# Twelve tiles of projection A per modulation block; the gate's modulation in the recurrence's weight stream

## The reference

```python
c_act = jax.nn.silu(c)                        # (1, 2048)
mod   = c_act @ ada_w[l] + ada_b[l]           # (1, 3*2048): shift | scale | gate
h     = rms_norm(x, pre_gain[l]) * (1.0 + scale) + shift
proj  = h @ w_in[l]                           # r,k,v | lora | z_a | conv, z_b | g_a, g_b
y_a   = (rwkv7_mix(pa, ...) * silu(z_a)) @ p_a[l]
y_b   = (short_conv_mix(pb, conv_w[l]) * silu(z_b)) @ p_b[l]
m     = sigmoid(g_a) * y_a + sigmoid(g_b) * y_b
x     = x + gate * rms_norm(m @ w_out[l], post_gain[l])
```

## Time and profile before

| | us |
|---|---|
| median of 3 runs (2261.99 to 2267.79) | 2263.99 |
| the profiled execution | 2260.67 |
| its span (first to last instruction) | 2259.1 |
| PE busy in it | 2211.5 |
| DVE busy | 1538.2 |
| ACT busy | 1106.0 |

### The profile page before, as it was taken

The page is one execution under the profiler, slowest core; times in us unless marked ns, Lnnn a source line. Parts: engine busy times, 40 slices in busy tenths (PEclk is TensorE's granted clock), DMA queues, the critical chain, the costliest instruction groups (busy, mean ns, idle before and its releaser), DMA issues.

```text
span 2259.1 us, 40660 instructions
## 1 busy us (share of the span) xinstructions
PE 2211.5 (98%) x15228; PEld 1869.7 (83%) x15228; DVE 1538.2 (68%) x2326; ACT 1106.0 (49%) x1741; POOL 123.3 (5%) x128
## 2 busy tenths in 40 slices
PE   6999999999999999999999999999999999999998
PEld 3688888888888888888888887888888888888887
DVE  5868776767776567678666666665566566566767
ACT  2344454555544456465455555544444454445454
POOL 0011000000000010120000002000000000000202
PEclk9999999999999999999999999999999999999999
DMA  9989744334334466665634435555555555555552
GB/s 377 390 314 352 248 138 136 124 132 132 122 122 134 151 228 219 219 205 177 205 131 131 141 126 191 184 178 194 178 194 183 190 177 195 182 189 183 182 184 84
DMA packets 116079, 424.86 MB, mean 188 GB/s; under 512 B 13200, under 2 KB 13456, under 8 KB 115696
## 3 DMA queue, kind: packets, MB, share of 16 engines
q1 hardware_dynamic: 107136, 390.68, 51.0%
q0 software_dynamic: 8816, 32.38, 4.1%
HBM read 414.62 MB, written 8.39 MB: 187 GB/s over the span
## 4 chain that ended last, share of the span: by engine, by line
PE 89%; DVE 5%; ACT 2%; DMA 2%; issue 1%; SPq 0%; DVEq 0%; ACTq 0%
PE ps L2102 48%; PE ps L2103 23%; PE ps L2220 5%; PE ps L2481 3%; PE ps L2482 1%; DMA raw<-in_stream 1%; DVE acc L1301 1%; DVE wlo L1270 1%; PE ps L2634 1%; ACT whi L700 1%; PE ps L2155 0%; DMA xt<-in_x 0%; PE ps L2156 0%; PE ps L2157 0%; DVE ysq L1536 0%
## 5 line engine op out<-in xcount | busy, mean ns | idle before, releaser
L2102 PE MATMUL ps<-acts,whi 128*128 128x512 f32 x3456 | 1254.4, 405 | 3.1 <-DVE stage L1276 1.6
L1270 DVE TENSOR_TENSOR wlo<-raw,whi 128x1024 fp32r<-128x1024 f32 x647 | 809.0, 1260 | 597.0 <-ACT whi L700 594.9
L700 ACT ACTIVATE whi<-raw 128x1024 fp32r<-128x1024 f32 x671 | 703.8, 1057 | 707.1 <-PE ps L2103 629.7
L2103 PE MATMUL ps<-acts,wlo 128*128 128x256 f32 x3456 | 967.5, 280 | 0.0
L2102 PEld LDWEIGHTS ps<-acts,whi 128*128 128x128 f32 x3456 | 649.3, 188 | 171.5 <-issue 9.1
L2103 PEld LDWEIGHTS ps<-acts,wlo 128*128 128x128 f32 x3456 | 652.9, 189 | 4.5 <-issue 3.3
L2102 PE MATMUL ps<-hidn,whi 128*128 128x512 f32 x1280 | 451.5, 397 | 2.3 <-DVE s L1276 1.8
L2103 PE MATMUL ps<-hidn,wlo 128*128 128x256 f32 x1280 | 357.2, 279 | 0.0
L2102 PEld LDWEIGHTS ps<-hidn,whi 128*128 128x128 f32 x1280 | 239.9, 187 | 63.9 <-DVE s L1276 4.2
L2103 PEld LDWEIGHTS ps<-hidn,wlo 128*128 128x128 f32 x1280 | 241.3, 188 | 0.5 <-issue 0.5
L700 ACT ACTIVATE half<-ps 128x256 f32<-128x256 f32 (+1 forms) x341 | 129.6, 386 | 77.7 <-PE ps L2103 50.7
(11 more groups left out here) (340 smaller groups left out, 2024.2 us busy)
## 6 DMA issues: line engine op xcount, KB each, us to landing
raw<-in_stream SPq DMA_DIRECT2D x735, 512.0 KB, 3.8
graw<-in_ada_gate POOLq DMA_DIRECT2D x32, 512.0 KB, 5.5
gate_dram<-stage POOLq DMA_DIRECT2D x32, 128.0 KB, 2.5
gab<-gate_dram POOLq DMA_DIRECT2D x8, 512.0 KB, 5.5
xt<-in_x SPq DMA_DIRECT2D x1, 2048.0 KB, 10.2
xt<-in_x POOLq DMA_DIRECT2D x1, 2048.0 KB, 9.4
ple_dram<-pr__111 POOLq DMA_DIRECT2D x4, 512.0 KB, 3.8
pj<-ple_dram POOLq DMA_DIRECT2D x1, 2048.0 KB, 12.4
```

Of the source, the lines that this page charges most:

```text
L700: return nc.scalar.activation(dst, src, ACT.Copy)
L1270: tt(wlo[:, n % SPLIT, :], raw[:, g % RAW, :], whi[:, n % SPLIT, :].bitcast(F32), ALU.subtract).then_inc(raw_used, 1)
L2102: mm(ps[bank + n][:, :], whi[:, n0 % SPLIT, c:c + P], act[:, off + kt + k, :], start=kt + k == 0, stop=False)
L2103: ins = mm(ps[bank + n][:, 0:T], wlo[:, n0 % SPLIT, c:c + P], act[:, off + kt + k, 0:T], start=False, stop=kt + k == last)
```

## The change

**Opening.** A block of the stream has 28 tiles instead of 22: 15 A (12 before), one P (four before) and 12 W (six before). With the six after the last block that makes 42 W tiles. They are 21 units of two tiles (`UNITS`: column block, quarter of the channels, pair of banks), and a pair of banks passes from one column block to the next: after the last unit of a partial sum ACT copies it to `rkvz` (`part_out`, 2 x 512 columns), and PE's next unit in these banks waits for that. The rest of projection A is 22 tiles in five pieces (`REST`: 6, 6, 4, 4 and 2 tiles); DVE puts each piece into `wt` and adds it to the part in `rkvz`, four small instructions more per piece. Neither the zeroing matmuls nor the copy of a row and its transposition are left: a P tile is now eight matmuls of a 128 x 128 piece of the tile with one column of `cact`, and the sum over `acc` eight of the same kind, straight into columns of bank 6. `modulation` stands one A tile earlier on DVE, `rows_lo` is in two halves, and ACT's `h` and `acts` go in two pairs.

**Gate.** The 32 tiles are part of the main stream, each just ahead of the weight tile that DVE splits at one of 32 chosen slots of the recurrence (`GATED`: three or four per stage, one in the last). `gate_sums` adds one with two DVE instructions of 512 columns just before that split, and `gate_columns` sums `gacc` on PE (4 matmuls) at slot 9 of stages 1, 3, 5 and 7. POOL loads none of them any more.

```diff
-WITH_ADA = "AAAAPAWPAWAPWAPWAAWAAW"
+WITH_ADA = "AAAA" + 6 * "AW" + "PAW" + 2 * "AAW" + "WWW"
 TAIL = 3
-OPEN = FIRST + 3 * WITH_ADA + "W" * 2 * EARLY
+UNITS = ((0, 0, 0), (1, 0, 1), (2, 0, 2), (3, 0, 0), (4, 0, 1), (5, 0, 2),
...
+REST = ((1, 2), (2, 2), (3, 4), (4, 4), (5, 6))
...
+GATED = {-1: (10, 20, 26), **{i: (5, 15, 21, 25) for i in (0, 2, 4, 6)}, **{i: (4, 10, 22, 26) for i in (1, 3, 5)}, 7: (4,)}
+GATES = sorted(LEAD + STAGE * (i + 1) + k for i, at in GATED.items() for k in at)
+GATE_AFTER = [WB0 + h // 2 - 1 + AHEAD for h in GATES]
...
-            with gp.Fori(0, 8) as i:
-                for m in range(4):
-                    gp.wait_ge(s.gate_used, i * 4 + (m + 1))
-                    gp.dma_start(graw[:, m, :], ada_gate[bass.ds(i * 4 + m, 1), :, :].rearrange("a p n -> (a p) n")
-                                 ).then_inc(gate_in[m], 16)
...
+            def part_out(w):
+
+                u = (w - SPLIT) // 2
+                if w % 2 == 0 or u not in ENDS[:-1]:
+                    return
+                blk_, _, at = UNITS[u]
+                act.wait_ge(quarters, used(WA0 + 2 * u + 1))
+                for n in range(2):
+                    p = blk_ % 2 * 4 + 2 * n
+                    copy(rkvz[:, p:p + 2, wa_at[blk_]:wa_at[blk_] + T], ps[2 * at + n][:, :].rearrange("p (a t) -> p a t", a=2)
+                         ).then_inc(s.part_out, 1)
...
-                for j in range(8):
-                    split(WA0 + 8 * b + j + AHEAD)
-                    if j < 7 and m < 2 * KT:
-                        dst = gacc[:, m // KT * CW:m // KT * CW + CW]
-                        dve.wait_ge(gate_in[m % 4], 16 * (m // 4 + 1))
-                        dve.wait_ge(s.gate_used, m + 4)
-                        stt(dst, graw[:, m % 4, :], cact[:, m % KT:m % KT + 1], dst, ALU.mult, ALU.add).then_inc(s.gate_used, 1)
...
+                for n in range(4):
+                    first_half(wt[:, n, :], n, 4 * EARLY + 4 * r + n)
+                for n in range(4):
+                    dve.wait_ge(evac_done, 4 * EARLY + 4 * r + n + 1)
+                    dst = rkvz[:, blk_ % 2 * 4 + n, wa_at[blk_]:wa_at[blk_] + T]
+                    V.do(tt(dst, dst, wt[:, n, :], ALU.add))
+                V.wait()
...
+            def gate_sums(m):
+                g, row = gate_place(m), m % 8 * 2
+                v = raw[:, g % RAW, :]
+                dve.wait_ge(raw_ready[g % RAW], 16 * (g // RAW + 1))
...
+                    stt(gacc[:, :], v[:, 0:512], cact[:, row:row + 1], gacc[:, :], ALU.mult, ALU.add).then_inc(s.gate_used, 1)
+                dve.wait_ge(s.gate_used, m + 1)
+                stt(gacc[:, :], v[:, 512:CW], cact[:, row + 1:row + 2], gacc[:, :], ALU.mult, ALU.add).then_inc(raw_used, 1)
...
                 def at(k):
-                    slot(LEAD + STAGE * (i + 1) + k)
+                    h = LEAD + STAGE * (i + 1) + k
+                    if h in GATES:
+                        gate_sums(GATES.index(h))
+                    slot(h)
...
-                for n in range(2):
-                    ins = mm(ps[6 + n][0:1, :], cact[:, j:j + 1], raw[:, g % RAW, n * 512:(n + 1) * 512], start=first, stop=False)
+                for n in range(8):
+                    ins = mm(ps[6][:, n:n + 1], raw[:, g % RAW, n * P:(n + 1) * P], cact[:, j:j + 1], start=first and n == 0, stop=False)
                 ins.then_inc(s.ada_used, 1)
...
-            for n in range(2 * EARLY):
-                mm(ps[n][:, :], ident, half[:, 0:2, :].rearrange("p a t -> p (a t)"), start=True, stop=False)
             sum_squares(0, scr0)
...
-            pe.wait_ge(s.gate_used, 36)
-            for n in range(KT):
-                ins = mm(ps[5][:, n:n + 1], gacc[:, n * P:(n + 1) * P], ones[:, 0:1], start=True, stop=True)
-            ins.then_inc(s.gate_ps, 1)
...
+            def gate_columns(p):
+                pe.wait_ge(raw_used, RAW + gate_place(8 * p + 7) + 1)
+                for n in range(4):
+                    ins = mm(ps[6][:, 448 + 4 * p + n:449 + 4 * p + n], gacc[:, n * P:(n + 1) * P], ones[:, 0:1], start=True, stop=True)
+                ins.then_inc(s.gate_ps, 1)
```

More of the change, by code:

```diff
@@ L173, in lay_out @@
         for kind, _, n in opening(b):
-            opened.append((w_a[n % (2 * EARLY) // 2, 2 * b + n % 2] if kind == "W" else shift_scale[b + 1][n])[None])
+            opened.append((w_a[UNITS[n // 2][0], 2 * UNITS[n // 2][1] + n % 2] if kind == "W" else shift_scale[b + 1][n])[None])
+    starts = [0] + [g + 1 - WB0 for g in GATE_AFTER]
     stream = [
         *opened,
-        w_a[EARLY:].reshape(-1, P, CW),
+        *[w_a[blk, j:] for blk, j in REST],
         w_in[:, 3 * DA:za].reshape(2, 8, P, P).transpose(0, 2, 1, 3).reshape(2, P, CW),
-        blocks(np.concatenate(conv_and_gates, 1)),
+        *[part for m in range(len(GATES)) for part in (w_b[starts[m]:starts[m + 1]], ada_gate[m:m + 1])],
+        w_b[starts[-1]:],
         *[blocks(p) for p in p_ab],
@@ L225, in opening, with in_stream, gate_place @@
     for n, kind in enumerate(kinds):
-        yield kind, at + n, 2 * EARLY * b + tile if kind == "W" else ada
+        yield kind, at + n, WITH_ADA.count("W") * b + tile if kind == "W" else ada
         ada, tile = ada + (kind != "W"), tile + (kind == "W")
+def in_stream(g):
+    return g + sum(after < g for after in GATE_AFTER)
+def gate_place(m):
+    return GATE_AFTER[m] + 1 + m
 def taken(g):
@@ L539, in block_of_two_layers @@
         eye = con[:, C_EYE:C_EYE + CH]
+        wa_at = [(OR, OK, OV, OZ)[blk_ // 2] for blk_ in range(8)]
         def per_chunk(c):
@@ L1340, in _ @@
                            ).then_inc(raw_used, 1)
-                    if n == 3 and b < 3:
+                    if n == 2 and b < 3:
                         modulation(b)
-                    if n == 8 and b < 3:
-                        rows_lo(b)
+                    if n in (3, 4) and b < 3:
+                        rows_lo(b, n - 3)
                     if n == 13 and b < 3:
                         rows_scaled(b + 1)
-            for w in range(8 * EARLY, 8 * EARLY + AHEAD):
+            for w in range(OPENED, OPENED + AHEAD):
@@ new lines, in _ @@
+            for r, (blk_, first) in enumerate(REST):
+                for j in range(first, 8):
+                    split(WA0 + w + AHEAD)
+                    w += 1
+                if r == 0:
+                    last, _, at = UNITS[-1]
+                    dve.wait_ge(quarters, 4 * (SPLIT + OPENED))
+                    dve.wait_ge(s.part_out, 2 * len(ENDS) - 2)
+                    for n in range(2):
+                        dst = rkvz[:, last % 2 * 4 + 2 * n:last % 2 * 4 + 2 * n + 2, wa_at[last]:wa_at[last] + T]
+                        tt(dst, ps[2 * at + n][:, :].rearrange("p (a t) -> p a t", a=2), dst, ALU.add).then_inc(evac_done, 2 * EARLY)
+                for n in range(4):
+                    first_half(wt[:, n, :], n, 4 * EARLY + 4 * r + n)
[4 more added lines that the diff above has]
+                V.wait()
@@ L1661, in _ @@
             centred(HT - 1)
+            gate_post()
             split(PAB0 + AHEAD)
```

179 lines of the change are left out of this document (90 added, 89 removed), and 3 rows, old and new, of the table UNITS.

## The result

| | before | changed |
|---|---|---|
| median of four runs each, us | 2262.99 (2259.95 to 2267.79) | 2239.19 (2238.54 to 2243.14) |
| the profiled execution, us | 2260.67 | 2238.54 |
| its span, us | 2259.1 | 2236.9 |

The ratio is 0.990, 95% interval 0.989 to 0.992: the kernel is faster by about 24 us in the medians and by 22.1 us in the profiled executions. Predicted were 2245 and a range of 2234 to 2256.

The account below looks back on a forecast made before the run. PE, busy for 2211.5 of 2259.1 us, was taken as the bound. Terms -20.5 - 3.0 + 3.6 + 2.0 + 0.4 = -17.5 on 2260.7 gave 2243.2, raised to 2245 for the runs' median; range 2234 to 2256.

Parts of the forecast that it names:

- rival 1: As forecast: PE the longest of three in the opening, 2245 us, own range 2238 to 2251; chance 0.62.
- the term -20.5: Change in when PE finishes projection A's 64 tiles, from 267.35 to 246.9 us; bounds -29 and -10.
- Start of the first W tile: In the opening: the first W tile starts at 49.5 us (48.58 before), bounds 45.5 and 52.
- The 42 W tiles and six short groups: Opening: 42 W tiles at 2.88 us, 121.0, plus three P tiles and three sums over `acc` at 2.0 each, 12.0.
- Waits and clock, 3 us: PE's waits and low clock in the opening's blocks: 3 us together, bounds 0 and 11; opened tiles done at 185.5.
- The other 22 tiles: Rest of projection A: 22 tiles at 2.79 us, 61.4 in all, ending at 246.9 us.
- Between projection A and the recurrence: Column sums and low clock go, 5.1 us; a wait for `xz` returns 2.1: -3.0, bounds -5.1 and 0.
- The recurrence: Column sums in four groups +3.6, gate sums' stalls +2 (bounds 0 and +12), `gate_post` behind the last stage +0.4 us.
- rivals, 2: No start penalty and no waits in the opening: 2231 to 2237 us; chance 0.13.
- Rival 3: DVE or the queues become the bound in the blocks, 41 us each instead of 38.6: 2252 to 2259; chance 0.13.
- Rival 4: The change does nothing: low clock after each of 11 one-column groups, 1.6 us each, 2260 to 2264; chance 0.08.
- Rival 5: Slower: gate sums push the recurrence's chain, sign turning at 0.6 us a sum; 2280 to 2290 at full 1.4; chance 0.04.

Follow-up runs that it names:

- e1: The kernel before with only the gate's move, its opening untouched: 2261.16 us, ratio 0.9995 to the kernel before.
- e9: The changed kernel run again with no edit, as direct partner of the runs beside it: 2242.95 us, ratio 0.991 to the kernel before.
- e11: The changed kernel with four P tiles per block, two W tiles after the sum over `acc`: 2258.71 us, ratio 0.9982 to the kernel before.
- e12: The changed kernel with no P tile in the blocks and DVE's two adds of the last partial sum moved behind the first split: 2237.98 us, ratio 0.9877.
- e3: The changed kernel without the product for the gate's modulation, the gate made of the bias alone: 2235.61 us, ratio 0.9884 to the kernel before.
- e5: The changed kernel with four P tiles per block, the first right behind the sum over `acc`: 2268.95 us, ratio 1.0014 to the kernel before.
- e6: The changed kernel with no P tile in the blocks, all 16 tiles of a block summed on DVE: 2240.57 us, ratio 0.9883 to the kernel before.
- e4: The changed kernel with two more 512-column DVE instructions ahead of each gate tile's sum: 2252.99 us, ratio 0.9955 to the kernel before.
- e8: The changed kernel with three wide matmuls behind the first block's column sums: 2245.15 us, ratio 0.9903 to the kernel before.

## Why the prediction was right, step by step

The mechanism was the one forecast (rival 1): PE the longest of three in the opening, the gate neutral. The prediction's four terms for the gate (-3.0 + 3.6 + 2.0 + 0.4) make its move 3.0 us dearer; by e1 it gains about 1, which leaves 19 to 21 us for the opening by the ratios. That is the size of the term -20.5, though a part of that one lies in waits and clock that no experiment took apart. Of the sum, -17.5, the profiled executions gave -22.1. The 4.6 us lie in these terms:

- *Start of the first W tile*, 49.5, bounds 45.5 and 52: 46.2 in the profiled execution, 49.4 in e9. The half clock in the P tiles was right, and so was the value for e9 and the other executions that start slowly. It was 3.3 us too late for this one; which start an execution gets is chance as far as the runs show, and the forecast was nearer to the slow one. One step was read wrongly: the sum of squares was taken at the 7.07 us that it has behind the zeroing, and standing first it took 8.61 and in e9 9.99.
- *The 42 W tiles and six short groups*: 2.87 us and 1.84 each, where 2.88 and 2.0 stood. 1.4 us too much; a P tile is 1.78 by e11.
- *Waits and clock, 3 us*: no waits at all, but 2.1 us of half clock up to 50.4, behind the long group. The modulation did fit into PE's three W tiles (8.6 us), although the prediction's own parts for it add up to 8.6 and not to 8.4. Together the opened tiles end at 179.9, not 185.5.
- *The other 22 tiles*, 61.4: they took 64.2. PE waited 1.26 us at 198.28 for `wt`, because two adds of 512 columns on the last partial sum stand ahead of the first piece's four. The prediction counted the four small adds and not these; e12 removes the wait. The rest is a pitch of 2.83 us, not 2.77, in three of the five pieces, and some 0.3 us at each piece's end. The sum took 2.79 from a single row of 2.77, while the kernel before needed 113.15 us for its 40 tiles there (154.20 to 267.35), 2.83 each. The whole term came out at -23.2 against -20.5.
- *Between projection A and the recurrence*: -4.1 against -3.0. The clock stays up, as said; the wait for `xz` was 0.85 and not 2.1 us.
- *The recurrence*, +6.0 in three terms: +5.1 from the lora product to the end. The column sums were 4 x 0.95 = 3.8. The stalls were mis-sized: 0.7 us more of waits than without a gate (e3), not 2, although a pair took 1.5 us and not 1.4.

Of the rivals, 2 (no start penalty, no waits) was half true, and the time fell between it and the forecast. Rival 3 is refuted by e5 and e11 for this number of P tiles; e6 shows that it starts one P tile further on. Rival 4, a low clock behind each group of one-column passes, does not hold for groups of 1.84 us between W tiles, but e5 shows it where two such groups stand with only an idle stretch of 1.7 us between them; whether the passes or the idle time did it there, the runs don't tell apart. At the start the clock fell in the passes alone: it was 0.71 from 26 to 28 us and 0.50 from there to the end of the sum, with PE busy throughout by the profile. The Trainium skill (TensorE: Matmul & The Clock Gate, Part 1) says that the gate goes by how busy the array has been recently. The trace agrees where PE had been idle (0.52 from 123.7 us in the kernel before, behind a wait of 2.12 us); in the passes of one column the profile shows PE as busy and the clock fell all the same, which that sentence by itself does not explain. Rival 5 needed 0.6 us per sum; e4 finds about 0.3 to 0.4 us per slot even for double the work.

## What to carry to other kernels

Where PE is busy for 98%, ask what fills it: the product of a 128 x 1024 tile with one vector cost PE 1.88 us as rows and 1.84 as columns, and 1.4 (e6) to 1.8 us (e11) a tile came back where another engine had the time for it. Work put in front of an engine's wait for a slower partner is nearly free up to the length of that wait (1.5 us a slot, e3), and beyond it a quarter of the work came through (e4). In this kernel one-column passes did no harm in short groups between W tiles: the same four P tiles per block cost 16 us in one order and 25 in another (e11, e5).

## What the hardware showed unexpectedly

- *PE's first passes are slow while the profile grants clock 1.00.* In e9 the 32 passes of the sum of squares take 9.99 us, in the profiled execution of the changed kernel 8.61, and in the earlier trace rows, behind the zeroing, 7.07. The instructions that start per window show where (changed kernel, then e9):

```profile
13.50:16.00 2.50, 2.38 (x6) 1.00 1.03 419
16.00:18.00 2.00, 2.00 (x10) 1.00 1.05 420
```

```profile
13.50:16.00 2.50, 2.37 (x6) 1.00 1.02 418
16.00:18.00 2.00, 2.00 (x6) 1.00 1.03 414
18.00:20.00 2.00, 2.00 (x7) 1.00 1.02 408
20.00:22.00 2.00, 2.00 (x11) 1.00 1.03 412
```

  From execution to execution this, and the moment at which the clock falls in the P tiles, moves the first W tile by 3.2 us; it stood at 46.2 to 46.7 in three profiles with the same start (the changed kernel, e3, e12) and at 49.4 to 49.7 in four (e4, e6, e8, e9). It may be much of the spread of the changed kernel's runs, 4.6 us, but only a profiled execution shows its start.
- *The same matmuls have two paces.* A pair of 512 and 256 columns (L2102 and L2103 and their like) stands 0.346 or 0.354 us from the next, 2.77 or 2.83 us a tile, by column block and by execution. In e1 the feed-forward ran in the slower one and took 730.1 us between VectorE's two reciprocals of `rs` (1447.22 and 2171.67 in the kernel before) where the kernel before took 724.5, with PE busy for 659.8 of 660 us. What sets the pace was not found; it means that one execution can't settle 5 us in this kernel.
